# Query products of a last norm made for the first 128 tokens ahead of the second 128

## Chip, core and metric

One core of a Trainium2 chip runs the kernel. The metric is the time of one execution in microseconds (us). Five engines work side by side and wait for each other by semaphores: TensorE (PE; matrix products, and PEld, its weight loads), VectorE (DVE), ScalarE (ACT), GpSimd (POOL) and SyncE (SP, which issues transfers).

## What is computed

The kernel is a network of three transformer-like layers on 256 tokens of width 1024. The change touches only the entry to its last part, a layer that picks experts per token:

```python
h = modulate_2(rms_norm(x, norm_ffn[l]), sh2, sc2)          # x * rstd * g * (1 + s) + shift
q = (hc @ w_query).reshape(B, T_CHUNK, PEER_HEADS, 2, PEER_DKEY // 2)   # 8 heads, two halves of 128
s = jnp.einsum('bthpd,hpnd->bthpn', q, sub_keys)            # 128 keys per half
s_top, i_top = lax.top_k(s, PEER_TOPK)                      # 16 best of each half
# 16 x 16 sums, the 16 best of them: e_idx (of 16384 experts), g = softmax
act = gelu(einsum('btd,bthkd->bthk', hc, u_emb[e_idx]))
out = einsum('bthk,bthkd->btd', g * act, v_emb[e_idx])
```

Each token and head takes 16 experts; for 256 tokens and 8 heads these are 256 gathers of 128 rows (one row per token, u and v side by side: 2048 float32 numbers), 1 MB each.

## The kernel before

The dense layers run first. They leave the sum x, transposed, in xT: eight pieces (kt = 0 to 7) of 128 channels by 256 tokens. The code has one function per engine, and each engine runs its instructions in the order in which that function issues them; nothing else orders the work but semaphores.

**The last norm ("ffn").** ACT squares each piece and scales it by the norm's weights into xa["ffn"] in HID (squares, scaled, L1371 and L1376). PE starts the query products before the root is known: raw_rows("ffn") multiplies the weights of the first head (two units, d = 0 and 1) by xa, 258 columns wide, of which the last two hold the shift, and adds over kt in banks 4 and 5 (L1929). After kt = 2 it makes the mean of the squares (mean_of_sum), and after kt = 5 it turns the root (L1938), so that rt holds one number per token. ACT takes the root (L1392). DVE then makes hp = root * shift + xa, which is h times the token's root, all 256 columns of a piece at once (L1143, eight instructions), the reciprocal of rt, the share of the shift (shift_share, L583) and the first head's queries pq, for tokens 0 to 127 (n = 0) and 128 to 255 (n = 1) (L1153).

**PE behind it.** turn_h(0) and turn_h(1) transpose hp for the first 128 tokens (L2367); key_scores(0) multiplies the queries of n = 0, then n = 1, by the keys (L2334); query(2) and query(3), key_scores(1), query(4), query(5), turn_h(2), turn_h(3), key_scores(2) follow; ten instructions of stand-in products (L1882); and then the mixes, mix(l) for l = 0 to 127, each two gathered rows by four instructions a row (L2344). The remaining queries stand between mixes.

**Choosing.** ACT copies key scores to SBUF (L1706). DVE runs route_steps, a generator: first_eight makes the best expert and then the best eight of the first head for n = 0 (L1176 to L1210), the next steps the remaining eight (L1266) and the gates (L1268, which waits for ACT's exponential, L1712). Then come the dots, dot(l) (L1282), with steps of the choice of later heads between them.

**Gathers.** POOL issues them in order (gather, L1843): row 0 waits for the best expert (s_eu8 = 1), rows 1 to 7 for the best eight, rows 8 and 9 for the rest of the head and for query(5) on PE, since their buffer row_h holds weights until then. Rows use ten buffers in turn (ring 4 and 5, row_x, HID twice, row_w, row_h) until row 80, fourteen later. Row 10 and all later ones wait until the row ten before has been mixed (s_mix). The two buffers in HID (rows 4 and 5) cover columns 1024 to 5119, where xa["ffn"] lies. SP issues one last 512 KB weight unit when the first head's raw products are done (L2481).

Of the kernel before, what the change touches and what calls it, by code (L numbers as in the profile page):

```python
# [8 lines left out]
ALU = mybir.AluOpType  # L9
# [70 lines left out]
def program(nc, A, out):  # L80
    es = ExitStack()
    with es:
# [3 lines left out]
        def sem(name):  # L86
            return es.enter_context(nc.semaphore(name))
# [129 lines left out]
        def raw_names(n):  # L217
            return [(*FIRST[n], d, 0) for d in range(2)]

        raw_bank = [ps[4], ps[5]]  # L220
        xa = {n: HID[:, at:at + 2064].rearrange("p (k t) -> p k t", k=8)
              for n, at in (("mlp0", 2048), ("conv", 5104), ("mlp1", 2048), ("b2", 2048), ("ffn", 2048))}
        a_of = {"mlp0": 1, "conv": 2, "mlp1": 3, "b2": 3, "ffn": 5}
        shifts = {n: sh[:, 2 * k:2 * k + 2] for k, n in enumerate(FIRST)}

# [6 lines left out]
        for name, b, kind, u in units:  # L232
            if kind == "rows":
                new = [(name, b, u, o) for o in range(2 if (name, b) == ("w_in", 3) else 1)]
                row_tiles += [] if first[name, b] + u in raw_pairs or first[name, b] + u in paced else new
            elif name == "w_out":
                new = [(name, b, u, o) for o in range(1 + apart(b, u))]
                row_tiles += new
            elif name == "w_out2":
                new = [(name, b, u, o) for o in range(1 + apart(b, u))]  # L240
                row_tiles += new
            elif kind == "toks" and u == 3:
                new = [(name, b, u, j) for j in range(4 if (name, b) == ("w_in", 4) else 2)]
            else:
                new = [(name, b, u)]
            if (name, b, u) in (("w_in", 1, 3), ("w_in2", 5, 3)):
                row_tiles += new
            if (name, b, u) == ("w_in", 0, 3):
                row_tiles += [("gmix", 0), ("gmix", 1)]
            dense_names += new  # L250
            used.append(new[-1])
        row_at = {name: i for i, name in enumerate(row_tiles)}
# [32 lines left out]
        def empty(name):  # L285
            if name[0] == "gmix":
                return g_out[name[1]]
            return out_a[name] if emptied_by(name) == "A" else out_v[name]
# [39 lines left out]
        def unit_in(i):  # L328
            if in_ring(i):
                return pair_in(i // 2)  # L330
            k = 2 if i == W0 + 15 else 0 if i in (W0 + 12, W0 + 13) else 1
            return s_late[k], (16, 48, 16)[k]
# [19 lines left out]
        xa_done = Steps(sem("act_x_scaled"), [(n, k) for n in FIRST for k in range(8)])  # L352
        shifted = Steps(sem("dve_shift_share"), [(n, d) for n in FIRST for d in range(2)])
        s_sig, s_sum = sem("act_first_gate"), sem("dve_last_squares")
        hp_done = Steps(sem("dve_h_by_root"), range(8))
        s_rt, s_rtd, s_pq = sem("pe_root_turned"), sem("dve_rstd_of_tokens"), sem("dve_first_queries")
        n_sc = Steps(sem("dve_scaled"), [(n, k) for n in hs for k in range(8)])
        n_hi = Steps(sem("act_h_hi"), [(n, k) for n in hs for k in range(8)])
# [147 lines left out]
        def dve():  # L506
# [67 lines left out]
                    shift_columns(n, M[:, layer, 24 * half:24 * half + 8])  # L574

            def shift_columns(n, b):
                affined.then_inc(ve.tensor_copy(xa[n][:, :, 256:258], b.unsqueeze(2).broadcast_to([128, 8, 2])), (n, "b"))

            def shift_share(n, d, bias=None):

                V.wait_ge(*dense[raw_names(n)[d]])
                s_, p = shifts[n][:, d:d + 1], raw_bank[d][:, 256:257]
                shifted.then_inc(ve.tensor_copy(s_, p) if bias is None else ve.tensor_tensor(s_, p, bias, ALU.add), (n, d))  # L583

            def norm(n, a, b, r, start=0, end=10):
# [552 lines left out]
                ve.tensor_tensor(s8[:, 0, :], s8[:, 0, :], s8[:, kt, :], ALU.add).then_inc(s_sum, 1)  # L1138
            V.wait_ge(*r_root["ffn"])
            root = rr[:, norms.index("ffn") % 2, :]  # L1140
            for kt in range(8):
                V.wait_ge(*xa_done["ffn", kt])
                hp_done.then_inc(ve.scalar_tensor_tensor(out=hp[:, kt, :], in0=root, scalar=M[:, 2, 24 + kt:25 + kt],  # L1143
                                                         in1=xa["ffn"][:, kt, 0:256], op0=ALU.mult, op1=ALU.add), kt)
            V.wait_ge(s_rt, 1)
            ve.reciprocal(rt[:], ps[1][:, 0:4]).then_inc(s_rtd, 1)
            for n in range(2):
                c = slice(128 * n, 128 * n + 128)
                for d, name in enumerate(raw_names("ffn")):
                    if n == 0:  # L1150
                        shift_share("ffn", d)
                        V.wait_ge(*shifted["ffn", d])
                    ins = ve.scalar_tensor_tensor(out=pq[:, d, c], in0=root[:, c], scalar=shifts["ffn"][:, d:d + 1],  # L1153
                                                  in1=raw_bank[d][:, c], op0=ALU.mult, op1=ALU.add)
                    if n:
                        out_v.then_inc(ins, name)
                    else:
                        ins.then_inc(s_pq, 1)


            def best16(vals, idx, src, work):
# [170 lines left out]

            route = route_steps()
            V.wait_ge(s_const, 5)
            for i in range(5):
                next(route)
            for l in range(128):
                dot(l)
# [16 lines left out]
        def act():  # L1355
# [17 lines left out]
            def scaled(n, kt):  # L1373

                S.wait_ge(*affined[n, "c" if n == "mlp0" and kt > 5 else "b"])
                xa_done.then_inc(se.activation(xa[n][:, kt, 0:256], xT[:, kt, :], ACT.Copy,  # L1376
                                               scale=ab[:, a_of[n], kt:kt + 1]), (n, kt))

            def squares(n, kts):

# [407 lines left out]
        def pool():  # L1788
# [57 lines left out]
            G.wait_ge(s_mod, NM)  # L1846
            gather(0)
            gather(1)
            gather(2)
            for l in range(3, 128):  # L1850
                if l == 4:
# [6 lines left out]
        def pe_():  # L1858
# [42 lines left out]
            def rows2(i, names, ready, hl):  # L1901
# [7 lines left out]
                for kt in range(8):  # L1909
                    T.wait_ge(*ready(kt))  # L1910
                    c = slice(kt * 128, kt * 128 + 128)
                    for d, name in enumerate(names):
# [5 lines left out]
                        if kt == 7:  # L1918
                            dense.then_inc(mm, name)

            def raw_rows(n):

                names, i = raw_names(n), raw_at[n]
                for d in range(2):
                    T.wait_ge(*unit_in(i + d))
                for kt in range(8):
                    T.wait_ge(*xa_done[n, kt])
                    for d in range(2):
                        mm = te.matmul(raw_bank[d][:, 0:258], unit_src(i + d)[:, kt * 128:kt * 128 + 128], xa[n][:, kt, :],  # L1929
                                       start=(kt == 0), stop=(kt == 7))  # L1930
                        if kt == 7:
                            dense.then_inc(mm, names[d])
                    if kt == (2 if n == "ffn" else 1):
                        mean_of_sum(n)
                    if kt == 5 and n == "ffn":
                        T.wait_ge(*r_root[n])
                        for t in range(2):
                            mm = te.matmul(ps[1][:, 2 * t:2 * t + 2], rr[0:1, norms.index(n) % 2, 128 * t:128 * t + 128],  # L1938
                                           ones[0:1, 0:2], start=True, stop=True)
                        mm.then_inc(s_rt, 1)  # L1940

            def toks_unit(w, b, u, outs, last=True):
                    i = first[w, b] + u
# [378 lines left out]
            for u in range(4):  # L2322
                out2_rows(1, u)

            def key_scores(h):
                for n in range(2):
                    if h == n == 0:
                        T.wait_ge(s_pq, 2)
                    for k in range(2) if h or n else ():
                        T.wait_ge(*empty(("wq", h // 2, 2 * (h % 2) + k, 0)))  # L2330
                    if h:
                        T.wait_ge(s_sc2, 2 * h + n - 1)
                    for k in range(2):
                        mm = te.matmul(ps[2 + n][:, k * 128:k * 128 + 128], pq[:, 2 * (h % 2) + k, n * 128:n * 128 + 128],  # L2334
                                       subk[:, 2 * h + k, :], start=True, stop=True)
                    mm.then_inc(s_scp, 1)
# [14 lines left out]
            def query(k):  # L2351
                name = ("wq", k // 4, k % 4, 0)
                T.wait_ge(*unit_in(W0 + k))
                T.wait_ge(*empty(row_tiles[row_at[name] - 2]))
                for kt in range(8):
                    T.wait_ge(*hp_done[kt])
                    mm = te.matmul(row_bank(name)[:, 0:256], unit_src(W0 + k)[:, kt * 128:kt * 128 + 128], hp[:, kt, :],  # L2357
                                   start=(kt == 0), stop=(kt == 7))
                dense.then_inc(mm, name)

            def turn_h(t):
                if t >= 2:
                    T.wait_ge(s_hn, t - 1)
                for k in range(4):
                    c, kt = slice(t // 2 * 128, t // 2 * 128 + 128), 4 * (t % 2) + k
                    T.wait_ge(*hp_done[kt])
                    mm = te.transpose(ps[6 + t % 2][:, k * 128:k * 128 + 128], hp[:, kt, c], ident[:])  # L2367
                mm.then_inc(s_hnp, 1)

            T.wait_ge(s_sub, 16)  # L2370
            raw_rows("ffn")
            turn_h(0)
            turn_h(1)
            key_scores(0)
            T.wait_ge(s_rtd, 1)
            query(2)
            query(3)
# [209 lines left out]
```

## Time and profile before

| | |
|---|---|
| median of 3 runs | 1522.09 us (1521.91 to 1522.61) |
| the profiled execution | 1522.05 us |
| its span in the trace | 1520.7 us |
| mean granted TensorE clock | 0.991 |
| busy: PE, PEld, DVE, ACT, POOL | 90%, 66%, 78%, 47%, 22% |
| chain that ended last | PE 52%, DMA 30%, DVE 10%, ACT 4% |
| gathers (q0) | 268.45 MB, 42.5% of 16 engines' span |

The span reaches from the first instruction to the last; the execution's own time has 1.35 us more around it. Busy shares are averages over stages that differ: to 850 us the dense layers keep PE at its work, from 861 us the gathers run. What a change at the border of the two is worth is read from the instructions there: who waits for whom, and when the transfers begin.

### The profile page before, as it was taken

Reading aid. Unit: us, or ns where it says so; the run is one execution under the profiler, and the core shown is the slowest. Engines: PE = TensorE matmul, PEld = TensorE weight load, DVE = VectorE, ACT = ScalarE, POOL = GpSimd, SP = SyncE. Lnnn points to the kernel's source line nnn. Section 1 sums busy time; section 2 is a strip of 40 time slices with the busy share of each in tenths; the row PEclk is TensorE's granted clock in tenths of the full one; section 3 lists DMA queues with packets and bytes.
Section 4 is the critical chain, followed back from the end, with each engine's and each line's share of the span. In section 5 each row is a group of like instructions: output and inputs, shape, how many; then the busy total and the mean of one; then the engine's idle time right before and its main releaser. Section 6 shows DMA issues by size and latency. Waiting matters only on the chain.

```text
span 1520.7 us, 20247 instructions
## 1 busy us (share of the span) xinstructions
PE 1374.4 (90%) x7310; PEld 1006.7 (66%) x7310; DVE 1188.6 (78%) x2402; ACT 720.7 (47%) x1636; POOL 341.6 (22%) x312
## 2 busy tenths in 40 slices
PE   8999999999999999999999999998787687877776
PEld 3878899999897999999888855444332232322222
DVE  6977888887998689897787787778877777767645
ACT  4555565456476755556354444333433343333322
POOL 1100100001000100003001354444644354434440
PEclk9999999999999999999999999999999899999999
DMA  9764369998530489994433699999999999999995
GB/s 388 316 243 161 144 224 357 361 351 312 208 126 1 167 330 369 349 343 160 167 111 139 238 422 422 420 422 421 420 422 421 422 421 421 422 422 421 422 421 243
DMA packets 66341, 477.12 MB, mean 314 GB/s; under 512 B 7361, under 2 KB 7361, under 8 KB 9153
## 3 DMA queue, kind: packets, MB, share of 16 engines
q0 software_dynamic: 36864, 268.45, 42.5%
q1 hardware_dynamic: 29376, 207.37, 36.5%
q8 instruction: 58, 0.95, 0.2%
q14 instruction: 41, 0.34, 0.1%
q10 hardware_dynamic: 2, 0.01, 0.0%
HBM read 474.75 MB, written 1.05 MB: 313 GB/s over the span
## 4 chain that ended last, share of the span: by engine, by line
PE 52%; DMA 30%; DVE 10%; ACT 4%; issue 2%; POOL 1%; ACTq 0%; DVEq 0%; POOLq 0%
DMA ring<-in_uv,crow 11%; DMA row_x<-in_uv,crow 9%; PE ps L2344 7%; PE ps L1896 5%; PE ps L1897 5%; PE ps L1898 5%; DMA HID<-in_uv,crow 5%; PE ps L2213 3%; DMA ring<-in_um 3%; PE ps L2216 3%; PE ps L2215 3%; PE ps L2240 3%; PE ps L2357 2%; DVE WB L537 2%; PE ps L1929 2%
## 5 line engine op out<-in xcount | busy, mean ns | idle before, releaser
L537 DVE TENSOR_TENSOR WB<-ring,WB 128x1024 fp32r<-128x1024 f32 x208 | 256.0, 1233 | 46.7 <-ACT WB L1366 44.6
L1366 ACT ACTIVATE WB<-ring 128x1024 fp32r<-128x1024 f32 x208 | 218.5, 1052 | 120.4 <-PE ps L2216 87.0
L1896 PE MATMUL ps<-hH,WB 128*128 128x256 f32 x752 | 216.1, 287 | 5.3 <-DVE WB L537 3.3
L2344 PE MATMUL ps<-ring,P 128*128 128x512 f32 x376 | 175.1, 611 | 46.0 <-ACT P L1727 46.0
L1898 PE MATMUL ps<-hH,WB 128*128 128x256 f32 x752 | 213.4, 284 | 0.0
L1897 PE MATMUL ps<-hL,WB 128*128 128x256 f32 x752 | 213.3, 284 | 0.0
L1717 ACT ACTIVATE On<-On 128x2 f32<-128x2 f32 x126 | 25.6, 203 | 358.7 <-DVE On L1282 358.6
L522 DVE CUSTOM_DVE_ANT_0 ring<-ring,crow,cols 128x1024 f32<-128x1024 f32 x128 | 163.7, 1281 | 20.0 <-DMA ring<-in_um 19.8
L2344 PEld LDWEIGHTS ps<-ring,P 128*128 128x128 f32 x376 | 69.7, 193 | 149.3 <-ACT P L1727 77.2
L1282 DVE CUSTOM_DVE_ANT_0 ring<-ring,cT 128x1024 f32<-128x1024 f32 x94 | 114.5, 1225 | 62.9 <-DMA ring<-in_uv,crow 62.2
L1896 PEld LDWEIGHTS ps<-hH,WB 128*128 128x128 f32 x752 | 144.7, 192 | 7.9 <-DVE WB L537 4.3
L1795 POOL TENSOR_TENSOR sq<-sq 128x256 f32<-128x256 f32 x30 | 31.4, 1047 | 518.4 <-ACT sq L1371 516.4
L2213 PE MATMUL ps<-XB,WB 128*128 128x256 f32 x512 | 145.2, 284 | 1.2 <-DVE WB L537 1.1
L2215 PE MATMUL ps<-XB,WB 128*128 128x256 f32 x512 | 144.9, 283 | 0.0
L2216 PE MATMUL ps<-XB,WB 128*128 128x256 f32 x512 | 144.9, 283 | 0.0
L1897 PEld LDWEIGHTS ps<-hL,WB 128*128 128x128 f32 x752 | 144.8, 193 | 0.1
L1898 PEld LDWEIGHTS ps<-hH,WB 128*128 128x128 f32 x752 | 144.7, 192 | 0.0
L1843 POOL DMA_INDIRECT ring<-in_uv,crow x94 | 101.6, 1080 | 136.6 <-PE ps L2344 108.8
L2344 PE MATMUL ps<-row_w,P 128*128 128x512 f32 x160 | 78.4, 635 | 25.7 <-ACT P L1727 25.7
L2213 PEld LDWEIGHTS ps<-XB,WB 128*128 128x128 f32 x512 | 98.2, 192 | 1.9 <-DVE WB L537 1.9
L2215 PEld LDWEIGHTS ps<-XB,WB 128*128 128x128 f32 x512 | 98.2, 192 | 0.0
L2216 PEld LDWEIGHTS ps<-XB,WB 128*128 128x128 f32 x512 | 98.2, 192 | 0.0
(353 smaller groups left out, 2899.1 us busy)
## 6 DMA issues: line engine op xcount, KB each, us to landing
ring<-in_stream SPq DMA_DIRECT2D x112, 1024.0 KB, 6.1
ring<-in_um SPq DMA_DIRECT2D x66, 1024.0 KB, 7.5
ring<-in_wm SPq DMA_DIRECT2D x4, 1024.0 KB, 12.8
bias<-in_bias SPq DMA_DIRECT2D x2, 2048.0 KB, 15.4
HID<-in_um SPq DMA_DIRECT2D x4, 512.0 KB, 18.3
row_h<-in_stream SPq DMA_DIRECT2D x2, 1024.0 KB, 8.0
ring<-in_uv,crow POOLq DMA_INDIRECT x94, 27.5
xT<-in_xT SPq DMA_DIRECT2D x1, 1024.0 KB, 8.9
```

The source lines that it names most:

```text
L522: ve.tensor_tensor_reduce(wk, wk, crow[:, layer // 2, :], 1.0, col[f"bm{layer}"][:, m:m + 1], ALU.mult, ALU.add, M[:, layer, m:m + 1]).the ...
L537: ve.tensor_tensor(unit_dst(j, 1), unit_src(j), f(unit_dst(j, 0)), ALU.subtract).then_inc(s_lo, 1)
L1282: ins = ve.tensor_tensor_reduce(u, u, hN[:, n, :], 1.0, 0.0, ALU.mult, ALU.add, dots[:, h, k0 + i:k0 + i + 1])
L1366: se.activation(unit_dst(j, 0), unit_src(j), ACT.Copy).then_inc(s_hi, 1)
L1843: nc.gpsimd.indirect_dma_start(row_ap[row_of[g]], None, A["uv"], bass.IndirectOffsetOnAxis(ap=eu[:, h, k0 + i:k0 + i + 1], axis=0)).then_i ...
L1896: te.matmul(o, wh[:, c], hi[:, kt, :], start=(kt == 0), stop=False)
L1897: te.matmul(o, wh[:, c], lo[:, kt, :], start=False, stop=False)
L1898: mm = te.matmul(o, wl[:, c], hi[:, kt, :], start=False, stop=(kt == 7))
L2213: te.matmul(o, wh[:, c], rH[d % 2][:, k, :], start=(d == 0 and h == 0 and k == 0), stop=False, skip_group_check=True)
L2215: te.matmul(o, wh[:, c], rL[d % 2][:, k, :], start=False, stop=False, skip_group_check=True)
L2216: mm = te.matmul(o, wl[:, c], rH[d % 2][:, k, :], start=False, stop=(d == 7 and k == 3), skip_group_check=True)
L2344: mm = te.matmul(ps[4 + 2 * n + q][:, :], diag[:, g % 8, :], row_ap[row_of[g]][:, 1024 + q * 512:1536 + q * 512], start=(g % 128 == 0), st ...
```

## The change

The raw products of the first head are cut by tokens. For n = 0, 130 columns (128 tokens and the two of the shift) are made for all kt, with the mean after kt = 5; then the root is turned, the first two kt of n = 1 are made, then the key scores of n = 0, then the remaining six kt of n = 1 (in bank 0), turn_h(0) and turn_h(1), and the key scores of n = 1. xa["ffn"] is written in the order tokens, shift, tokens for that (xa_first), and the shift's columns move to 128 and 129.

DVE makes the queries of n = 0 before any of hp, then the reciprocal and half of the first tokens' hp (4 pieces of 128 columns), then first_eight, and only then the other 4 pieces, the 8 pieces of n = 1, and the queries of n = 1. The hp instructions become 16 of 128 columns in place of 8 of 256. POOL waits for the queries of n = 1 before it issues gather(2) (rows 4 and 5), since DVE and PE read xa until then.

```diff
+            def h_by_root(n, kts):
+                c = slice(128 * n, 128 * n + 128)
+                for kt in kts:
+                    V.wait_ge(*xa_done["ffn", kt])
+                    hp_done.then_inc(ve.scalar_tensor_tensor(out=hp[:, kt, c], in0=root[:, c], scalar=M[:, 2, 24 + kt:25 + kt],
+                                                             in1=xa_first[kt][:, n, :], op0=ALU.mult, op1=ALU.add), (n, kt))
+
+            first_queries(0)
+            V.wait_ge(s_rt, 1)
+            ve.reciprocal(rt[:], ps[1][:, 0:4]).then_inc(s_rtd, 1)
+            h_by_root(0, range(4))
...
             route = route_steps()
             V.wait_ge(s_const, 5)
-            for i in range(5):
+            next(route)
+            h_by_root(0, range(4, 8))
+            h_by_root(1, range(8))
+            first_queries(1)
+            for i in range(4):
                 next(route)
...
             gather(1)
+            G.wait_ge(*out_v[raw_names("ffn")[1]])
             gather(2)
...
+            def first_pair(n, kts):
+                c = slice(130 * n, 130 * n + (128 if n else 130))
+                for kt in kts:
+                    T.wait_ge(*xa_done["ffn", kt])
+                    for d in range(2):
+                        o = ps[0][:, 128 * d:128 * d + 128] if n else raw_bank[d][:, 0:130]
+                        mm = te.matmul(o, unit_src(W0 + d)[:, kt * 128:kt * 128 + 128], xa["ffn"][:, kt, c],
+                                       start=(kt == 0 and not n * d), stop=(kt == 7), skip_group_check=bool(n))
...
+                if n == "ffn":
+                    first_pair(0, range(6))
+                    mean_of_sum(n)
+                    first_pair(0, range(6, 8))
+                    T.wait_ge(*r_root[n])
+                    for t in range(2):
+                        mm = te.matmul(ps[1][:, 2 * t:2 * t + 2], rr[0:1, norms.index(n) % 2, 128 * t:128 * t + 128],
+                                       ones[0:1, 0:2], start=True, stop=True)
+                    mm.then_inc(s_rt, 1)
+                    first_pair(1, range(2))
+                    return
...
             raw_rows("ffn")
+            key_scores(0, (0,))
+            first_pair(1, range(2, 8))
             turn_h(0)
             turn_h(1)
-            key_scores(0)
+            key_scores(0, (1,))
+            T.wait_ge(*empty(("wq", 0, 1, 0)))
             T.wait_ge(s_rtd, 1)
             query(2)
```

## Rows read from the trace of the kernel before

**Rows 1.** The page's slices: GB/s moved in each of 40 slices of 38.0 us.
```profile
GB/s 388 316 243 161 144 224 357 361 351 312 208 126 1 167 330 369 349 343 160 167 111 139 238 422 422 420 422 421 420 422 421 422 421 421 422 422 421 422 421 243
```

**Rows 2.** Chain that ended last: start us, us, what (x instructions).
```profile
848.34 2.62 PE ps L1929 x12
...
854.00 0.53 PE ps L1938 x4
...
856.47 0.87 PE ps L2367 x8
857.34 1.06 PE ps L2334 x8
858.41 6.92 PE ps L2357 x32
...
874.75 0.89 PE ps L2334 x8
875.64 4.29 PE ps L1882 x10
879.94 13.93 PE ps L2344 x32
...
920.60 15.35 DMA row_w<-in_uv,crow
...
1482.04 28.17 DMA row_x<-in_uv,crow
```

**Rows 3.** Timeline of ACT and DVE: start us, us, instruction, [idle before <-releaser].
```profile
851.42 0.47 ACT L1392 ACTIVATE rr<-ps,eps 128x256 f32<-128x256 f32 x1 [1.71 <-PE ps L1873]
...
857.93 0.47 ACT L1706 ACTIVATE HID<-ps,rt 128x256 f32<-128x256 f32 x1 [6.03 <-PE ps L2334]
...
868.79 0.31 ACT L1712 ACTIVATE On<-crow,On 128x16 f32<-128x16 f32 x1
...
851.93 3.26 DVE L1143 SCALAR_TENSOR_TENSOR xN<-rr,M,HID 128x256 f32<-128x256 f32 x8 [2.16 <-ACT rr L1392]
...
856.07 0.16 DVE L583 COPY sh<-ps 128x1 f32<-128x1 f32 x1 [0.79 <-PE ps L1929]
...
856.71 0.86 DVE L1153 SCALAR_TENSOR_TENSOR HID<-rr,sh,ps 128x128 f32<-128x128 f32 x3
858.50 0.30 DVE L1176 MAX8 crow<-HID 128x8 f32<-128x128 f32 x1 [0.92 <-ACT HID L1706]
...
862.61 0.17 DVE L1210 CAST crow<-crow 128x7 uint32<-128x7 f32 x1
...
871.61 0.17 DVE L1266 CAST crow<-crow 128x8 uint32<-128x8 f32 x1
```

**Rows 4.** Timeline of POOL: issues of rows 0, 4, 8 and 10.
```profile
861.12 1.09 POOL L1843 DMA_INDIRECT ring<-in_uv,crow  x1 [12.43 <-DVE crow L1190]
...
866.80 0.94 POOL L1843 DMA_INDIRECT HID<-in_uv,crow  x1 [0.30 <-issue]
...
874.15 1.04 POOL L1843 DMA_INDIRECT row_h<-in_uv,crow  x1 [2.43 <-PE ps L2357]
...
881.92 1.24 POOL L1843 DMA_INDIRECT ring<-in_uv,crow  x1 [5.49 <-PE ps L2344]
```

**Rows 5.** Windows: length, busy PE, PEld, DVE, ACT, POOL, then PEclk, DMA share, GB/s.
```profile
862.50:863.00 0.50, 0.50 (x5) 0.42 (x4) 0.47 (x4) 0.00 (x0) 0.00 (x0) 1.00 0.51 115
...
862.00:884.00 22.00, 21.48 (x92) 15.18 (x91) 20.73 (x72) 10.39 (x27) 10.63 (x12) 1.00 0.96 382
```

**Rows 6.** PE's timeline ahead of two falls of the clock, and windows behind them.
```profile
1100.36 4.11 PE L2344 MATMUL ps<-row_w,P 128*128 128x512 f32 x5 [2.21 <-ACT P L1727]
...
1100.00:1105.00 5.00, 4.64 (x7) 2.03 (x8) 3.07 (x8) 1.41 (x6) 0.94 (x1) 0.66 1.02 423
...
1210.86 6.69 PE L2344 MATMUL ps<-row_w,P 128*128 128x512 f32 x8 [6.45 <-ACT P L1727]
...
1210.90:1216.90 6.00, 6.00 (x7) 2.46 (x8) 5.75 (x15) 2.13 (x7) 1.09 (x1) 0.50 1.02 423
```

More of the change, by code:

```diff
@@ L222, in program @@
               for n, at in (("mlp0", 2048), ("conv", 5104), ("mlp1", 2048), ("b2", 2048), ("ffn", 2048))}
+        xa_first = [HID[:, 2048 + 258 * k:2308 + 258 * k].rearrange("p (n t) -> p n t", n=2)[:, :, 0:128] for k in range(8)]
         a_of = {"mlp0": 1, "conv": 2, "mlp1": 3, "b2": 3, "ffn": 5}
@@ L249, in program @@
                 row_tiles += [("gmix", 0), ("gmix", 1)]
+            if name == "wq" and (b, u) == (0, 0):
+                dense_names += [("wq", 0, d, 0, "first tokens") for d in range(2)]
             dense_names += new
@@ L354, in program @@
         s_sig, s_sum = sem("act_first_gate"), sem("dve_last_squares")
-        hp_done = Steps(sem("dve_h_by_root"), range(8))
+        hp_done = Steps(sem("dve_h_by_root"), [(n, k) for n in range(2) for k in range(8)])
         s_rt, s_rtd, s_pq = sem("pe_root_turned"), sem("dve_rstd_of_tokens"), sem("dve_first_queries")
@@ L576, in shift_columns @@
             def shift_columns(n, b):
-                affined.then_inc(ve.tensor_copy(xa[n][:, :, 256:258], b.unsqueeze(2).broadcast_to([128, 8, 2])), (n, "b"))
+                c = slice(128, 130) if n == "ffn" else slice(256, 258)
+                affined.then_inc(ve.tensor_copy(xa[n][:, :, c], b.unsqueeze(2).broadcast_to([128, 8, 2])), (n, "b"))
             def shift_share(n, d, bias=None):
-                V.wait_ge(*dense[raw_names(n)[d]])
-                s_, p = shifts[n][:, d:d + 1], raw_bank[d][:, 256:257]
+                V.wait_ge(*dense[("wq", 0, d, 0, "first tokens") if n == "ffn" else raw_names(n)[d]])
+                at = 128 if n == "ffn" else 256
+                s_, p = shifts[n][:, d:d + 1], raw_bank[d][:, at:at + 1]
                 shifted.then_inc(ve.tensor_copy(s_, p) if bias is None else ve.tensor_tensor(s_, p, bias, ALU.add), (n, d))
@@ L1140, in dve, with first_queries @@
             root = rr[:, norms.index("ffn") % 2, :]
[L1141 to L1147, printed above, removed]
+            def first_queries(n):
                 c = slice(128 * n, 128 * n + 128)
@@ L1152, in dve @@
                         V.wait_ge(*shifted["ffn", d])
+                    elif d == 0:
+                        V.wait_ge(*dense[raw_names("ffn")[1]])
                     ins = ve.scalar_tensor_tensor(out=pq[:, d, c], in0=root[:, c], scalar=shifts["ffn"][:, d:d + 1],
-                                                  in1=raw_bank[d][:, c], op0=ALU.mult, op1=ALU.add)
+                                                  in1=(ps[0][:, 128 * d:128 * d + 128] if n else raw_bank[d][:, 0:128]), op0=ALU.mult, op1=ALU.add)
                     if n:
@@ L1375, in scaled @@
                 S.wait_ge(*affined[n, "c" if n == "mlp0" and kt > 5 else "b"])
-                xa_done.then_inc(se.activation(xa[n][:, kt, 0:256], xT[:, kt, :], ACT.Copy,
-                                               scale=ab[:, a_of[n], kt:kt + 1]), (n, kt))
+                dst, src = xa[n][:, kt, 0:256], xT[:, kt, :]
+                if n == "ffn":
+                    dst, src = xa_first[kt], src.rearrange("p (n t) -> p n t", n=2)
+                xa_done.then_inc(se.activation(dst, src, ACT.Copy, scale=ab[:, a_of[n], kt:kt + 1]), (n, kt))
             def squares(n, kts):
@@ L1919, in rows2 @@
                             dense.then_inc(mm, name)
+            def first_pair(n, kts):
[6 more added lines that the diff above has]
+                                       start=(kt == 0 and not n * d), stop=(kt == 7), skip_group_check=bool(n))
+                        if kt == 7:
+                            dense.then_inc(mm, ("wq", 0, d, 0) if n else ("wq", 0, d, 0, "first tokens"))
             def raw_rows(n):
@@ L1925, in raw_rows @@
                     T.wait_ge(*unit_in(i + d))
+                if n == "ffn":
+                    first_pair(0, range(6))
[8 more added lines that the diff above has]
+                    return
                 for kt in range(8):
@@ L1932, in raw_rows @@
                             dense.then_inc(mm, names[d])
-                    if kt == (2 if n == "ffn" else 1):
+                    if kt == 1:
                         mean_of_sum(n)
[L1935 to L1940, printed above, removed]
             def toks_unit(w, b, u, outs, last=True):
@@ L2323, in pe_, with key_scores @@
                 out2_rows(1, u)
-            def key_scores(h):
-                for n in range(2):
+            def key_scores(h, halves=(0, 1)):
+                for n in halves:
                     if h == n == 0:
@@ L2355, in query @@
                 for kt in range(8):
-                    T.wait_ge(*hp_done[kt])
+                    T.wait_ge(*hp_done[1, kt])
                     mm = te.matmul(row_bank(name)[:, 0:256], unit_src(W0 + k)[:, kt * 128:kt * 128 + 128], hp[:, kt, :],
@@ L2365, in turn_h @@
                     c, kt = slice(t // 2 * 128, t // 2 * 128 + 128), 4 * (t % 2) + k
-                    T.wait_ge(*hp_done[kt])
+                    T.wait_ge(*hp_done[t // 2, kt])
                     mm = te.transpose(ps[6 + t % 2][:, k * 128:k * 128 + 128], hp[:, kt, c], ident[:])
```

## The prediction

> **What bounds the kernel now.** I read three views. First, the slices of the page [rows 1]: from the 24th slice to the last but one the DMA engines move 420 to 422 GB/s, and the 256 expert rows of the last stage (128x2048 f32, 1.049 MB each) are nearly all of it, so a row costs 2.49 us. The end of the kernel is then the start of this stream, plus 256 rows, plus every hole in it. Second, the chain of waits around the last norm [rows 2]: it runs on TensorE (PE) without a break from 848.34 through the query products to the first mix at 879.94, and near the end of the kernel it stands in a transfer that queues for 28.17 us. So past 920 the mixes are early and the transfers set the pace; a row issued at 920.60 already takes 15.35 us to land. Third, the issues on GpSimd (POOL) [rows 4] beside the DMA windows [rows 5]. Row 0 is issued at 861.12 as soon as VectorE (DVE) has the best expert. There are ten buffers: row 10 needs buffer 0 back and is issued at 881.92, 1.98 us after mix 0 starts. So two things can set the stream: the first choice, and the first mix.
>
> How near is the second? By 884.00 the stream has moved 22 x 382 GB/s = 8.40 MB, 8.0 rows; of ten, 2.0 are left, 4.9 us, so row 9 ends at 888.9. From the first issue at 861.12 to the first bytes (a mean of 115 GB/s in 862.5 to 863.0, so they begin inside it; I take 862.7) are 1.6 us; row 10 could deliver from 883.5. **Its slack is 5.4 us.** Rows 8 and 9 (issued from 874.15, the last query of the first four) have 8.2 us.
>
> **Part 1, first choice earlier.** The raw products change from 258 columns to 130 and then 128. An instruction of 258 columns takes 2.62/12 = 0.218 us; one of 128, 0.89/8 = 0.111 [rows 2]; one of 130 I take at 0.1125. Before the mean stand now 24 of these, 2.70 us, in place of 12, 2.62: the mean and the root (851.42, rows 3) move by +0.1. Then 8 instructions (0.9) end the first half at 852.37, where now it is 856.47: 4.1 earlier. DVE's shift share and two products take from 856.07 to about 857.05 [rows 3]; the same 1 us puts them at 853.2. PE meanwhile turns the root (0.53) and makes 8 instructions of the second half (0.89) before the key scores, which start at 853.79 against 857.34: these 8 hide the wait for DVE and cost about 0.6 more. The first choice moves by **-3.55**: ScalarE's (ACT) copy starts 0.59 behind the key scores, now at 857.93, then at 854.38, DVE's MAX8 from 858.50 to 854.95. DVE has before it the reciprocal and four pieces of h; 256 columns take 3.26/8 = 0.41, 128 columns from PSUM 0.29; a 128-column piece from SBUF lies between half of 0.41, 0.20, and 0.29; I take 0.28, so they end at 854.5, under the copy. Rows 0 and 1 are issued 3.55 earlier, at 857.57. The new wait of POOL ahead of rows 4 and 5 is for DVE's second queries: 862.61+0.1-3.55 = 859.15 is the end of the first choice, then 12 pieces of h (3.36) and two products (0.57) make 863.1, where without a wait these rows come at 866.80-3.55 = 863.25. The wait is hidden, by 0.15 only; behind it stand rows 4 to 7 and all later gathers, but eight rows are 20 us of transfer, so a few tenths vanish. The last 512 KB weight unit on SP goes at 857, 0.4 later, and falls on the first row: some tenths, hidden as well.
>
> **Part 2, what PE now waits for.** The second key scores need DVE's second queries, 863.1, and so do queries 2 and 3, behind them on PE. Today query 2 begins at 858.41 [rows 2]. After: key scores at 863.1, 0.44 for four, query 2 at 863.5: **+5.1 us**. Nothing in PE's order from there to mix 0 is taken away: queries 2 to 5, their key scores, the turns and the ten stand-in products (4.29) are one unbroken chain. Mix 0 goes from 879.94 to 885.0. ACT's order is the same and moves along. DVE gets a new stall: the reciprocal of the first gates (behind 871.61) needs ACT's exponential, now at 868.79, which stands on ACT behind the key scores of the second head; with them it moves by the 5.1, to 873.9, and ends some 0.5 later, while DVE is there at 872.0, so DVE stands some 2.4 us and its dots come that much later, still less than PE's 5.1. It costs nothing alone: the mixes after it are later still.
>
> Row 10: +5.1 - 5.4 = -0.3. So even with the clock held the gain of 3.55 is gone: the stream starts early, runs out of its ten rows at 885.3 and waits for the first mix. Starting anew is not free: today the first bytes come at 862.7 but the 8.0 rows by 884 count back to 864.1, 1.4 lost in a ramp with few rows in flight. Between 0 and 1.4 I take **+0.8**, since rows 10 and on are issued at the mixes' pace (13.93/8 = 1.74 us each), as thin as rows 0 and 1 were.
>
> **The clock.** Behind the first key scores (854.23) PE has 24 products of 0.111 and the first turn of h (0.44), so it stands idle from 857.3 to 859.4, makes four transposes as DVE hands over pieces (0.9 us), and idles again from 860.3 to 863.1: some 4.9 us idle in 5.8. In this trace the granted clock fell to half (1.2 of 2.4 GHz) after much the same: after idle time of 2.21 us ahead of 1100.36, and of 6.45 us ahead of 1210.86 [rows 6]. In the first case it was low 0.34 x 5 x 2 = 3.4 us, which takes 1.7 us of work; in the second the engine worked 6.0 us at half, 3.0 lost. I take **+2.5**, nearer the second, as the idle here is as long as that one's. The queries and everything up to mix 0 take it in full. The Trainium skill (TensorE: Matmul & The Clock Gate, "HAM oscillation — how this bites in real kernels") asks that no single idle gap between bursts reach a length that it states; both gaps here are shorter, so by that rule the clock would hold and the sum would be +0.5. The row ahead of 1100.36, with a gap of 2.21, disagrees; the rule's outcome is rival B.
>
> **Sum.** +5.1 (PE waits for the second queries) - 5.4 (slack of row 10) + 2.5 (clock) + 0.8 (ramp) = **+3.0 us**. After row 10 nothing adds: rows 10 and on are issued 1.74 apart and served 2.49 apart, so the queue fills again, and the row issued at 920.60 has 15.35 - 1.6 - 2.5 = 11 us in hand, more than any delay here. The profiled execution took 1522.05 us (span 1520.7, 1.35 around it), the median of the runs is 1522.09; so 1525.1.
>
> **Rivals.**
> A, the forecast: the stream runs dry before row 10 with the clock fallen, 1525.1; its own range is 1523.8 to 1526.5 (clock 1.7 to 3.0, ramp 0 to 1.4). For it: two idle stretches close together in an engine whose clock fell after 2.21 us. 52%.
> B, the clock holds: 5.1 - 5.4 + 0.8 = +0.5, 1522.6 (1521.7 to 1523.2). For it: the transposes in the middle, and the page's rule. Against it: the row at 1100.36. 20%.
> C, the first choice alone decides, since row 10 has more slack than I count or PE catches up: -3.55, 1518.5. It needs PE's delay to be under 1.9 us, or a slack of 9 and more. Against: the unbroken chain from 858.41 to 879.94. 11%.
> D, slower: the stream stops twice. With the clock low for the longest case, queries 4 and 5 end late, and row 8, which waits for query 5 (874.15 today), comes at 874.15+5.1+3.3 = 882.5, first bytes at 884.1, while eight rows are through at 888.9-3.55-2x2.49 = 880.4; a hole of 3.7 and a second ramp. It decides once PE's delay at query 5 is over 8.2-3.55 = 4.7 us, but the price is only the second ramp where row 10 is late too: 5.1 - 5.4 + 3.3 + 1.4 + 1.4 = +5.8, 1527.9. 15%.
> The remaining 2% is that the change doesn't bring the first choice forward (ACT's copy held up by something not seen): the delay stays, above 1525.
>
> **Chances.** What a measurement of this kernel can tell from no change is about 0.2%, 3.0 us: below 1519.05 or above 1525.13. Faster is C less its upper edge, 0.10. Of A, whose centre is at the bound, somewhat over half lies within: same is 0.29 of A, 0.20 of B, 0.01 of C: 0.50. Slower is 0.23 of A, 0.15 of D and the rest: 0.40. The range for 8 in 10 takes A and B whole and half of D: 1521.0 to 1527.4.
>
> **What the profile of after would show.** Row 0 issued 3.5 us earlier relative to the last residual; PE idle in two pieces before the second key scores, query 2 about 5 us later; PEclk below 1 in the microseconds behind it; DMA below 420 GB/s in a hole 20 us or so after the first row; row 10 issued at 889 to 890 with mix 0 starting at 887.5. If mix 0 is at 885 with the clock at 1.00, it is B. If there is no hole, C. Wrong in the step would be a piece of h that costs over 0.35 us or under 0.2 (12 of them: 1 us on all of PE's delay).

## The result

| kernel | median | ratio to before, 95% interval |
|---|---|---|
| before | 1522.01 us (20 runs) | |
| changed | 1524.32 us (20 runs) | 1.0016 [1.0010, 1.0023] |

The change costs 2.3 us (1.5 to 3.5). 1525.1 was forecast, by a stream of gathers that starts earlier, runs dry, and is set by the first mix in place of the first choice. The trace shows this picture. The page of the changed kernel, GB/s in 40 slices of 38.1 us; the 24th slice, which covers 876 to 914 us, is the one to compare with [rows 1]:

```profile
GB/s 389 321 236 165 140 231 350 359 353 311 211 122 1 166 342 374 346 344 154 155 111 156 276 346 421 421 421 421 421 422 421 422 421 421 421 421 422 421 421 252
```

It moved 422 GB/s before and moves 346 now, and the slice ahead of it 276 in place of 238: the early bytes are there (38 GB/s more), and about twice as much is missing behind them (76 GB/s less). The later slices are alike but for the last, in which the longer kernel still moves its rest (252, before 243).

In this execution the norm begins 0.84 us earlier than in the one of before (first raw product at 847.50, before 848.34 [rows 2]), which is scatter of the dense layers ahead, so I compare distances from it. The chain of waits of the changed kernel (start us, us, what):

```profile
847.50 2.68 PE ps L1948 x24
...
853.13 0.46 PE ps L2371 x4
...
858.52 3.14 DVE xN L1166 x12
861.66 0.53 DVE HID L1155 x2
...
862.32 1.19 PE ps L2371 x4
863.51 9.24 PE ps L2394 x32
...
873.26 1.13 PE ps L2371 x8
...
883.07 4.29 PE ps L1903 x10
887.36 13.73 PE ps L2381 x32
```

The first key scores come at 853.13, and now a stretch of DVE stands in the chain: the 12 pieces of h and the two second queries, behind which PE's second key scores wait until 862.32. Then the key scores take 1.19 us for four instructions and queries 2 and 3 take 9.24 us, where 32 of them took 6.92 [rows 2]. PE's timeline has two idle stretches ahead of them, 2.13 and 2.38 us long, with four transposes between:

```profile
858.83 1.11 PE L2404 MATMUL ps<-ident,xN 128*128 128x128 f32 x4 [2.13 <-DVE xN L1166]
862.32 1.19 PE L2371 MATMUL ps<-bias,HID 128*128 128x128 f32 x4 [2.38 <-DVE HID L1155]
```

The windows (length, busy PE, PEld, DVE, ACT, POOL, PEclk, DMA share, GB/s) say why the work behind them is slow, and show the two holes in the transfers:

```profile
862.00:868.00 6.00, 5.68 (x16) 4.72 (x17) 5.52 (x26) 0.47 (x1) 4.48 (x6) 0.50 0.98 377
881.00:884.00 3.00, 3.00 (x21) 2.40 (x20) 2.93 (x8) 2.60 (x6) 2.12 (x2) 1.00 0.09 19
890.00:892.00 2.00, 2.00 (x6) 0.84 (x5) 1.90 (x7) 0.00 (x0) 1.22 (x2) 1.00 0.49 98
```

From 862 to 868 the granted clock is half (it was 1.00 up to 861 and 0.63 in 861 to 862, so it fell within the second idle stretch). From 881 to 884 nearly nothing moves (19 GB/s): eight rows are through and row 8 is not there. From 890 to 892 the same once more ahead of row 10. POOL's issues of rows 0, 4, 8 and 10, to be held against [rows 4], and DVE's new stall:

```profile
856.87 1.09 POOL L1863 DMA_INDIRECT ring<-in_uv,crow  x1 [9.02 <-DVE crow L1204]
...
864.02 0.94 POOL L1863 DMA_INDIRECT HID<-in_uv,crow  x1 [0.30 <-issue]
...
881.57 1.65 POOL L1863 DMA_INDIRECT row_h<-in_uv,crow  x1 [12.88 <-PE ps L2394]
...
889.35 0.94 POOL L1863 DMA_INDIRECT ring<-in_uv,crow  x1 [4.89 <-PE ps L2381]
...
876.65 0.16 DVE L1282 RECIPROCAL On<-On 128x1 f32<-128x1 f32 x1 [5.60 <-ACT On L1732]
```

Row 0 is 861.12 - 856.87 - 0.84 = 3.41 us earlier after the norm's start, row 4 stands behind its new wait without idle time (0.30 is issue), rows 8 and 10 wait for PE and come 8.3 us later after the norm's start.

In the experiments below, one execution of the kernel with 2.57 us more on PE took 4804.93 us for an unknown reason; the intervals leave it out, and the median is the same with it.

### The profile page after: what moved, and what is told of

It is laid out like the page before. It is cut to its first block, busy times and chain, and to the rows that moved or that the text cites. A ratio compares the mean times of both kernels' runs of the same rounds, so it can differ in the third digit from the quotient of the medians.

```text
span 1523.4 us, 20319 instructions
## 1 busy us (share of the span) xinstructions
PE 1375.1 (90%) x7342; PEld 1009.4 (66%) x7342; DVE 1187.9 (78%) x2410; ACT 720.3 (47%) x1636; POOL 339.7 (22%) x312
## 4 chain that ended last, share of the span: by engine, by line
PE 58%; DMA 25%; DVE 9%; ACT 5%; issue 2%; POOL 1%; ACTq 0%; DVEq 0%; POOLq 0%
PE ps L2381 10%; DMA ring<-in_uv,crow 10%; DMA row_x<-in_uv,crow 9%; PE ps L1917 6%; PE ps L1918 6%; PE ps L1919 6%; DMA HID<-in_uv,crow 4%; PE ps L2250 4%; PE ps L2253 4%; PE ps L2252 4%; PE ps L2394 3%; PE ps L2277 3%; DMA ring<-in_um 2%; DVE WB L540 2%; PE ps L1972 1%
```

## The experiments

Two sizes tell the kernels apart, both counted from the norm's first raw product, since executions differ by several us in the layers ahead: when POOL issues row 10, and when the queue of the gathers has moved its first 40 rows (worked out from the trace's transfer records, good to about 0.1 us; past the 16th row the difference from the kernel before stays within 0.3 us up to the 240th in every kernel). Both sizes are of the one profiled execution of each kernel, and are given as differences from the kernel before; the ratios are over all executions, those of an experiment against runs of the kernel before on the same chip. The kernel before has row 0 at 12.95, row 10 at 33.75, 40 rows at 115.98.

| kernel | median us, ratio [95%] | row 0 | row 10 | 40 rows |
|---|---|---|---|---|
| changed | 1524.32, 1.0016 [1.0010, 1.0023] | -3.42 | +8.26 | +4.27 |
| changed, again | 1524.08, 1.0010 [0.9999, 1.0021] | -3.42 | +6.96 | +3.15 |
| late start | 1526.27, 1.0031 [1.0018, 1.0044] | +2.17 | +9.32 | +5.39 |
| gaps filled with stand-ins | 1522.49, 1.0012 [1.0000, 1.0023] | -3.42 | +5.43 | +1.52 |
| gaps filled with queries, 1st | 1523.32, 1.0008 [0.9998, 1.0017] | -3.42 | +8.06 | +4.72 |
| the same, 2nd | 1519.29, 0.9988 [0.9979, 0.9997] | -3.43 | +2.52 | -1.26 |
| the same, 3rd | 1519.77, 0.9983 [0.9973, 0.9992] | -3.42 | +1.78 | -2.03 |
| before + 2.57 us on PE | 1522.52, 1.0007 [0.9997, 1.0018] | 0 | +2.58 | +0.06 |
| before + 5.15 | 1524.42, 1.0016 [1.0007, 1.0025] | 0 | +6.27 | +2.35 |
| before + 7.72 | 1525.22, 1.0027 [1.0018, 1.0036] | 0 | +7.73 | +3.67 |
| before, weight unit late | 1522.88, 1.0015 [1.0006, 1.0024] | 0 | 0 | +1.36 |

**PE's delay alone.** Stand-in products on PE in the kernel before, without the early start:

```diff
             key_scores(0)
+            stand_in(ps[5], cols[:, 0:512], 6)     # 3 and 9 in the others
             T.wait_ge(s_rtd, 1)
             query(2)
```

> The kernel before with six stand-in products (twelve instructions, 5.15 us) on TensorE ahead of query 2, with no idle time and no fall of the clock: this is the change's delay on TensorE alone, without its early start. Theory (row 10 has 5.4 us of slack): mix 0 is 5.15 us later and the kernel 0 to 0.8 us slower. Rival 1 (TensorE's chain sets the end): +5.15. Rival 2 (more slack than counted): 0, and no hole in the transfers.

> The kernel before with three stand-in products (2.57 us) on TensorE ahead of query 2. Theory (slack of 5.4 us at row 10): row 10 is issued 2.6 us later and no hole opens; the time is the kernel before's, 0 +-0.5. Rival (every delay of TensorE here counts): +2.6.

> The kernel before with nine stand-in products (7.72 us) ahead of query 2. Six of them (5.15) cost 2.9 us, where 0 to 0.8 was expected; in that trace row 10 came 6.3 us later than its distance to row 0 was before, and rows 9 to 12 took 2.4 us longer. Theory, slack of 5.4 and a ramp of up to 1.4: 7.7 to 8.8 - 5.4 + 1.4 = +3.7 to +4.8. Rival (no slack, TensorE's delay in full): +7.7 or more. Three, six and nine together give the bend: flat, then one for one.

2.57 us move nothing in the stream (+0.06 at 40 rows; no hole), as expected. The time alone could not say so: it is 1522.52, +1.5, and its interval (-0.5 to 2.7) holds both the theory's 0 and the rival's +2.6. 5.15 cost more than I expected, 2.35 in the trace and 2.9 in time (1.1 to 3.8); 7.72 cost 3.67 and 4.2, at the lower end of what was expected. The bend is there: the last two, and three kernels of other making, lie on one line, row 10's delay less 4.0 (6.27 - 3.92, 7.73 - 4.06, 5.43 - 3.91, 8.26 - 3.99, 9.32 - 3.93). So 4.0 us of delay are free. That fits the 5.4 us counted as slack with the ramp of 1.4 paid in full, but the line gives only the difference of the two: a smaller slack and a smaller ramp would lie on it just as well. The window in which row 10 is awaited with 7.72 us more, and the same with 2.57:

```profile
884.00:888.00 4.00, 4.00 (x11) 1.74 (x10) 3.90 (x11) 3.40 (x14) 0.00 (x0) 1.00 0.97 379
```

```profile
884.00:888.00 4.00, 4.00 (x11) 1.75 (x10) 3.86 (x11) 0.56 (x3) 2.44 (x3) 1.00 1.01 422
```

In the kernel with 5.15 us, row 10 came 6.27 later and not 5.15: ACT took query 3 only at 874.35, while PE's rows have it end at 873.19. In the kernel before ACT takes it within 0.04 us of that end.

```profile
874.35 0.38 ACT L1405 ACTIVATE HID<-ps 128x256 f32<-128x256 f32 x1 [4.19 <-PE ps L2357]
```

The last section comes back to that.

**The early start alone.** GpSimd's new wait moved ahead of the very first gather:

```diff
             G.wait_ge(s_mod, NM)
+            G.wait_ge(*out_v[raw_names("ffn")[1]])
             gather(0)
             gather(1)
-            G.wait_ge(*out_v[raw_names("ffn")[1]])
```

> The changed kernel with one edit: GpSimd waits for the second queries ahead of the very first gather, not ahead of the third pair, so rows 0 to 7 are issued some 5.3 us later (row 0 near 862.2 in place of 856.9) and nothing on TensorE changes. Theory (the first mix gates row 10 and with it the stream; the early start buys nothing): the time stays that of the changed kernel, 0 to 0.6 us under it because the two holes close and one ramp is saved; about +2 us on the kernel before. Rival (the stream is set by its start): the time grows by the 5.3 us, to some +7.5 on the kernel before.

Row 0 is 5.6 us later than in the changed kernel, 2.2 later than in the one before. The stream follows row 10 as on the line above (9.32 - 3.93 = 5.39) and knows nothing of row 0; the rival's +7.5 is excluded. The expected 0 to 0.6 us from one saved ramp didn't appear, and the hole ahead of row 10 stayed (336 GB/s over 888 to 892). The time is 1526.27, 4.8 us over the kernel before (2.7 to 6.7), where the changed kernel was 2.3 over it: 1.1 of the difference of 2.5 is row 10, which this execution issues 1.06 us later (again a late signal for query 3); the rest is inside the interval. The early start of the change buys nothing as long as the first mix is that late.

**The clock.** Stand-in products in PE's two gaps:

```diff
             turn_h(0)
+            stand_in(ps[5], cols[:, 0:512], 2)
             turn_h(1)
+            stand_in(ps[5], cols[:, 0:512], 2)
             key_scores(0, (1,))
```

> The changed kernel with two stand-in products (four instructions, 1.7 us) in each of TensorE's two idle gaps, ahead of the second turn of h and ahead of the second key scores; no wait is changed. Theory: the granted clock stays at 1.00 around 860 to 870, the key scores and queries 2 and 3 take 0.5 and 6.9 us again in place of 1.2 and 9.2, mix 0 starts about 3 us earlier (near 884.5), row 10 is issued near 886.5, and the kernel takes about 1522.5, +0.5 on the kernel before and 2 under the changed one. Rival (the fall of the clock is beside the point, the time is lost in DVE's stall or in the new waits): it stays at +2.3.

Timeline of PE, and a window over it, of this kernel:

```profile
859.37 1.12 PE L2404 MATMUL ps<-ident,xN 128*128 128x128 f32 x4 [0.41 <-DVE xN L1166]
...
862.87 0.68 PE L2371 MATMUL ps<-bias,HID 128*128 128x128 f32 x4 [0.66 <-DVE HID L1155]
863.39 7.07 PE L2394 MATMUL ps<-xN,row_h 128*128 128x256 f32 x32
```

```profile
856.00:872.00 16.00, 14.41 (x69) 10.30 (x68) 14.57 (x65) 2.92 (x6) 7.92 (x8) 1.00 0.85 308
```

The clock stays at 1.00, queries 2 and 3 take 7.07 us in this view, as in the kernel before (9.44 in the changed one), row 10 comes 2.8 us sooner than in the changed kernel, and the stream gains those 2.75 us (4.27 - 1.52). The time is 1522.49, +1.0 on the kernel before (0 to 3.5), where +0.5 was expected. This is rival B's case, at about B's price, and the fall of the clock costs the changed kernel's profiled execution 2.8 us.

**PE's gaps filled with work.** Queries 2 and 3 are made in halves by tokens, and the second half of the raw products goes to bank 3 (query_part, not shown, makes query k for the tokens of one n from the named pieces; DVE reads bank 3 accordingly):

```diff
             turn_h(0)
-            turn_h(1)
-            key_scores(0, (1,))
-            T.wait_ge(*empty(("wq", 0, 1, 0)))
             T.wait_ge(s_rtd, 1)
-            query(2)
-            query(3)
+            for k in (2, 3):
+                query_part(k, 0, range(4))      # first tokens, pieces 0 to 3
+            turn_h(1)
+            for k in (2, 3):
+                query_part(k, 0, range(4, 8))
+            query_part(2, 1, range(8))
+            key_scores(0, (1,))
+            query_part(3, 1, range(8))
...
-                        o = ps[0][:, 128 * d:128 * d + 128] if n else raw_bank[d][:, 0:130]
+                        o = ps[3][:, 128 * d:128 * d + 128] if n else raw_bank[d][:, 0:130]
```

> The changed kernel with TensorE's gaps filled by real work: queries 2 and 3 are made for the first 128 tokens in two parts of four pieces (behind the first and behind the second turn of h), then for the second 128; the second half of the first head's raw products goes to bank 3 so that query 2's bank is free. The same products are made. Theory: query 3 ends only some 1 us later than in the kernel before, mix 0 near 881, row 10 inside its slack of 5.4 us, so that the start of the stream decides: 3.4 us under the kernel before, about 1518.6. DVE's wait for the exponential is gone too. Rival (the early start can't be kept, since the queue refills at the mixes' pace in any case): 1521.5 or more.

The first measurement was a miss: 1523.32, +1.8 on the kernel before (-0.3 to 2.6), where -3.4 was expected. Its timelines of ACT and PE, and a window behind them:

```profile
869.06 0.47 ACT L1726 ACTIVATE sq<-ps,rt 128x256 f32<-128x256 f32 x1 [8.26 <-remote]
...
863.48 0.61 PE L2371 MATMUL ps<-bias,HID 128*128 128x128 f32 x4
863.93 1.95 PE L2404 MATMUL ps<-xN,row_h 128*128 128x128 f32 x16
870.18 2.04 PE L2371 MATMUL ps<-bias,HID 128*128 128x128 f32 x8 [4.30 <-ACT HID L1425]
```

```profile
869.00:876.00 7.00, 5.82 (x18) 5.04 (x19) 3.49 (x11) 3.65 (x8) 0.00 (x0) 0.54 1.01 427
```

PE's gaps are closed up to 865.9, as planned. But ACT copies the second key scores, which PE starts at 863.48 and has behind it at 863.93, only at 869.06: 5.1 us in which no engine is named that held it. PE idles for its answer, and the clock falls. This kernel is also 0.6 us off the line (8.06 - 3.34 = 4.72): behind row 10 its rows 11 to 13 are issued up to 0.4 us later than in the changed kernel, and row 10's own issue takes 1.68 us in place of 0.94, which is of that size; no run tests it. The same kernel was measured twice more, each time on another chip.

> The same kernel as the one with TensorE's gaps filled by halves of queries 2 and 3, once more, to see whether its wait of ScalarE (key scores ended at 863.93 on TensorE, copied at 869.06, 5.1 us late, with TensorE idle for 4.3 and its clock at half behind that) is part of the kernel or of that one execution. If it is of one execution: the trace shows the copy within 0.1 us of the key scores, key scores of the second head near 866.5, row 10 issued near 882, no hole in the transfers, and a time 1 to 2 us under the kernel before (the early start of 3.4 less some 1.25 for the last weight unit's 0.52 MB, which now falls into the stream). If it is of the kernel: the same late copy, and 1 to 2 us over the kernel before.

> The kernel with TensorE's gaps filled by halves of queries 2 and 3, a third time, since its first measurement came out 1.8 us over the kernel before (one 5.1 us late signal from TensorE to ScalarE in its trace) and its second 1.8 us under (no such wait). Theory (the delay belongs to single executions): 1 to 2.1 us under the kernel before, from -3.4 for the start and +1.3 for the weight unit in the stream; row 10 issued less than 2.6 us later after the norm's first product than in the kernel before. Rival (the filled order brings the late signal on in most executions): 1 to 2 us over.

In both, the copy of the key scores is on time and ACT sees query 3 late by only 1.3 and 0.5 us, row 10 comes 2.5 and 1.8 us later, no hole like those above opens, and the kernel is 1.8 and 2.1 us faster than the one before (0.5 to 3.2, and 1.2 to 4.1). Windows and issue of row 10 of the third:

```profile
881.00:884.00 3.00, 3.00 (x9) 1.32 (x8) 2.83 (x11) 1.80 (x7) 0.00 (x0) 1.00 1.01 421
889.00:892.00 3.00, 3.00 (x8) 1.33 (x7) 2.90 (x8) 1.46 (x6) 2.24 (x2) 1.00 1.01 418
```

```profile
884.31 1.70 POOL L1863 DMA_INDIRECT ring<-in_uv,crow  x1 [5.60 <-PE ps L2381]
```

In the third measurement the start does decide: 40 rows are moved 2.03 us earlier. That is not the 3.4 of row 0; the difference is the next experiment. In the second they are moved only 1.26 us earlier, and there row 10 still decides: a stream that is 2.06 us ahead (the next experiment has this figure) also runs out 2.06 us earlier, so of the 4.0 us of free delay 1.9 are left. Row 10's 1.78 us in the third are within them, its 2.52 us in the second are not (2.52 - 3.95 = -1.43, against -1.26 found). The first measurement differs from the other two by more than the intervals, so the gain holds for two of three; as each was made on another chip, the chip is not excluded as the cause of the difference.

**The weight unit.** In the kernel before, the last 512 KB unit is issued behind query 3, at 865.16 in place of 856.55:

```diff
-            for j in range(W0, W0 + 2):
+            for j in range(W0, W0 + 4):
                 P.wait_ge(*dense[used[j]])
             sp.dma_start(unit_src(W0 + 15), A["stream"][L0 + 7][:, 1024:2048]).then_inc(s_late[2], 16)
```

> The kernel before with the transfer of the last 512 KB weight unit held back until query 3 is made (issued near 865.4 in place of 856.55), so that it runs beside the gathers as in the changed kernel, and not ahead of them. Theory: the stream is later by its bytes, 0.524 MB at 422 GB/s = 1.2 us: +1.2 us, and the eighth row's transfer ends 1.2 us later relative to the first issue. Rival (it fits into the ramp, where the engines are not full): 0 to 0.4.

40 rows are moved 1.36 us later (0.52 MB at 422 GB/s are 1.2), and the time is 1.8 us up (0.9 to 3.7). In the kernel before this transfer lies in an idle stretch of the DMA engines ahead of the first gather. An earlier first gather moves into it: -3.42 + 1.36 = -2.06, against -2.03 in the third measurement of the filled kernel.

**The changed kernel again.**

> The changed kernel itself on the same chip and between the same runs. Theory: 2 to 4 us over the kernel before and 4 to 5 over the filled one; in its trace the delay of row 10's issue since the norm's first product, less 3.95, is the delay of the 40th row's landing, as it was in five kernels (6.27 gave 2.35, 7.73 gave 3.67, 5.43 gave 1.52, 8.26 gave 4.27, 9.32 gave 5.39). Rival (that line was chance): the difference is off by more than 0.5.

It took 1524.08, 2.2 over the kernel before (-0.2 to 3.2) and 4.3 over the filled one, measured on the same chip. Here row 10 is 6.96 late: the clock was at half for a shorter stretch, and queries 2 and 3 took 8.1 us in PE's timeline, not 9.4:

```profile
867.57 8.13 PE L2394 MATMUL ps<-xN,row_h 128*128 128x256 f32 x32
```

By the line, 6.96 - 3.95 = 3.01, and 3.15 was found.

## Why the prediction was right

- **The first choice, -3.55.** -3.41 in the trace. Products of 130 columns took 2.68/24 = 0.112 us, forecast 0.1125; pieces of h 0.26 to 0.28 (3.14 for 12), forecast 0.28.
- **POOL's new wait hidden by 0.15.** Row 4 has no idle time in front of it, so the wait is hidden. Row 4 still comes 1.6 us later after the norm's start than forecast (864.02 + 0.84 = 864.86, against 863.25), since the issue of row 2 took 2.32 us and not 0.94, for which I have no cause. It is without weight, since row 10 decides.
- **PE waits, +5.1.** The second key scores start 14.8 us after the norm's start (862.32 - 847.50), forecast 863.1 - 848.34 = 14.8; with full speed behind them query 2 would be 5.2 late.
- **The clock, +2.5.** It fell in both executions of the changed kernel, though by the Trainium skill's rule on single gaps (TensorE: Matmul & The Clock Gate, "HAM oscillation — how this bites in real kernels") it would have held with gaps of 2.13 and 2.38 us. The key scores lost 0.7 and queries 2 and 3 lost 2.3: 3.1 in the first execution; in the second 1.8 (6.96 - 5.2). The two executions lie at the two ends of the range of 1.7 to 3.0.
- **Slack of row 10, 5.4, and the ramp, +0.8.** This is the term that came out wrong: together 4.0 us of delay are free, not 5.4 - 0.8 = 4.6. If the slack is as counted, the ramp is 1.4, its upper bound; that the fault lies in the ramp alone is not shown. The second measurement of the filled kernel speaks against so neat a division: against its earlier stream row 10 is 2.52 + 2.06 = 4.6 us late, under 5.4, and 0.8 us are lost all the same (-1.26 in place of -2.06).
- **"Some tenths, hidden as well" for the weight unit.** Wrong by size, 1.36 us; that it is hidden is right, since where row 10 decides these bytes only go ahead of the hole: kernels with the unit in the stream (5.43, 8.26) and without it (6.27, 7.73, 9.32) lie on the same line.
- **Sum.** With measured terms: 5.2 + 3.1 - 4.0 = +4.3 at the 40th row of the first execution, 1.3 more than forecast (0.1 of it the wait, 0.6 the clock, 0.6 the ramp). From the norm's start to the last instruction this execution was only 3.6 us longer than the one of before, the second execution of the changed kernel 2.4; over 20 runs it is +2.3. The difference comes behind the 240th row: to the end of the gathers the first execution took 46.5 us, the one of before 47.3. That isn't the change's doing as far as the traces show, since the stretch lies between 46.3 and 47.7 in the twelve profiled executions, and the longest is one with the order of before. That 3.0 was so near is in part luck: terms too small by 1.3 against a scatter of the clock's fall (1.8 in the other execution) and of the end. Also, A's own range (1523.8 to 1526.5) leaves out row 10's -0.3; its terms give 1523.5 to 1526.2, and 1524.32 lies in either.
- **Rivals.** D's picture, two holes, came at A's price: a hole ahead of row 8 costs nothing by itself when row 10 is late anyway. C failed: the late start has the same 4.0 between row 10 and the stream as the changed kernel, whatever row 0 does. With another order on PE it came true in one measurement, at -2.0 and not -3.55. DVE's stall was 5.6 us long, forecast 2.4 with the clock held (2.8 in the kernel with stand-ins), and cost nothing: PE runs without a break through it to mix 0 (883.07 to 887.36 in the chain above).

## What to carry to other kernels

A stream of transfers over a ring of buffers has two gates: its first issue, and the first reuse of a buffer. Before making the first earlier, count the slack of the second, from what is still queued when the reuse is issued, less the ramp that an empty queue pays, and less the head start itself, by which the queue also runs out sooner. Here 5.4 us were counted and 4.0 were free. And look at what lay in the gap into which the stream is moved: other transfers, and an engine's work that kept its clock up; real work by halves can fill it.

## What the runs showed of the hardware

- Two idle stretches of PE of 2.1 and 2.4 us with 1.1 us of work between them were followed by half the granted clock in all three profiled executions with this order (the changed kernel twice, and the late start), and it fell within the second stretch; the same order with 0.4 and 0.7 us of idle time kept 1.00. The Trainium skill (TensorE: Matmul & The Clock Gate, "HAM oscillation — how this bites in real kernels") counts single gaps, by which none of this would fall; here the measurement decides.
- In six of the profiled executions something that PE had finished by its rows was seen late by ACT: query 3 by 0.5 to 1.3 us in four (5.15 us more on PE, late start, and the filled kernel's 2nd and 3rd), query 4 by 2.6 us with the weight unit late (where nothing waited for it, since PE was busy with query 5), and the key scores by 5.1 us once, where ACT's record names no instruction as the releaser. In the filled kernel the key scores of the second head came about 1 us late as well; row 10 did not hang on them. In each of the six the trace has the increment of the semaphore itself late (869.03 for those key scores, which PE's rows end by 864.1), so it is not ACT that slept; the ends of PE's instructions are modelled, so its work may have ended later than its rows say. The instruction queues moved nothing from 863.4 to 882.8 in the execution with 5.1 us, so it was no load of instructions that the trace shows. The wait came and went between executions of one kernel, on different chips. Its cause is open; nothing here was tried on it. It is large enough, with the clock's fall behind it, to turn the filled kernel from 1519.3 to 1523.3: row 10's delay is 8.06 us with it and 2.52 without.
